# Four shift columns in the high operand, and the norm's sum of squares by one product with ones, in a two-layer diffusion-transformer step

## What is computed

```
h = rms_norm(x, g_mix) * (1 + scale1) + shift1
mo, k, v = mixer(h, w_in, ...)            # differential attention | short convolution, then w_out
x = x + gate1 * mo
h = rms_norm(x, g_ffn) * (1 + scale2) + shift2
x = x + gate2 * ffn(h)                    # SwiGLU in layer 0, top 2 of 8 experts in layer 1
```

## Time and profile before

| | |
|---|---|
| median of 3 runs | 1975.42 us (1972.21 to 1979.14) |
| profiled execution, its own time | 1974.79 us |
| its span | 1972.9 us |
| PE busy | 1910.0 us, 97% of the span, 12579 matmul rows |
| DVE busy | 1117.6 us, 57% |
| ACT busy | 803.2 us, 41% |
| POOL busy | 122.2 us, 6% |
| granted TensorE clock, mean | 0.99 |

### The profile page before, as it was taken

The page is one execution under the profiler, slowest core; times in us unless marked ns, Lnnn a source line. Parts: engine busy times, 40 slices in busy tenths (PEclk is TensorE's granted clock), DMA queues, the critical chain, the costliest instruction groups (busy, mean ns, idle before and its releaser), DMA issues.

```text
span 1972.9 us, 30669 instructions
## 1 busy us (share of the span) xinstructions
PE 1910.0 (97%) x12579; PEld 1748.1 (89%) x12579; DVE 1117.6 (57%) x1799; ACT 803.2 (41%) x1331; POOL 122.2 (6%) x102
## 2 busy tenths in 40 slices
PE   8999889999999999999999899899999999999997
PEld 6999768999999999999997588899898988989885
DVE  2643776444332344437347754476676766768577
ACT  4221364322211222222213644455565655656564
POOL 2000000100000000110000001220000000002210
PEclk8999999999999999999998999899999999999999
DMA  9525100324231431305252011577686776768762
GB/s 348 183 79 205 62 1 22 108 97 181 76 118 43 176 124 65 124 27 192 81 199 53 1 44 39 144 231 244 218 250 212 223 241 204 246 201 303 256 196 73
DMA packets 91699, 290.49 MB, mean 147 GB/s; under 512 B 13236, under 2 KB 21812, under 8 KB 91552
## 3 DMA queue, kind: packets, MB, share of 16 engines
q1 hardware_dynamic: 84416, 270.15, 41.2%
q0 software_dynamic: 7136, 18.30, 2.9%
HBM read 281.98 MB, written 12.28 MB: 149 GB/s over the span
## 4 chain that ended last, share of the span: by engine, by line
PE 90%; DVE 5%; ACT 2%; issue 2%; DMA 1%; SPq 0%; DVEq 0%; ACTq 0%
PE ps L706 47%; PE ps L1056 12%; PE ps L1045 12%; PE ps L1046 6%; PE ps L766 2%; PE ps L891 2%; PE ps L1049 2%; PE ps L882 1%; DVE pr L1995 1%; DVE nbias L1971 1%; PE ps L1048 1%; PE ps L739 1%; DMA ada_raw<-ada_w 1%; PE ps L898 1%; PE ps L1120 1%
## 5 line engine op out<-in xcount | busy, mean ns | idle before, releaser
L1734 DVE TENSOR_TENSOR w_lo<-raw,w_hi 128x1024 fp32r<-128x1024 f32 x394 | 485.2, 1233 | 385.4 <-ACT w_hi L1226 375.7
L1226 ACT ACTIVATE w_hi<-raw 128x1024 fp32r<-128x1024 f32 x394 | 414.4, 1053 | 343.4 <-PE ps L706 172.3
L1045 PE MATMUL ps<-hg,w_hi 128*128 128x416 f32 x1232 | 380.7, 366 | 2.0 <-DVE hg L2152 1.8
L706 PE MATMUL ps<-a_hi,w_hi 128*128 128x320 f32 x1472 | 343.3, 314 | 3.4 <-DVE a_lo L1776 3.4
L706 PE MATMUL ps<-a_lo,w_hi 128*128 128x320 f32 x1472 | 341.0, 313 | 0.0
L706 PE MATMUL ps<-a_hi,w_lo 128*128 128x320 f32 x1472 | 339.9, 312 | 0.0
L1046 PE MATMUL ps<-hg,w_lo 128*128 128x208 f32 x1232 | 319.9, 260 | 0.0
L706 PEld LDWEIGHTS ps<-a_hi,w_hi 128*128 128x128 f32 x1472 | 249.8, 191 | 11.2 <-issue 7.4
L706 PEld LDWEIGHTS ps<-a_hi,w_lo 128*128 128x128 f32 x1472 | 250.9, 190 | 0.0
L706 PEld LDWEIGHTS ps<-a_lo,w_hi 128*128 128x128 f32 x1472 | 250.1, 190 | 0.0
L1045 PEld LDWEIGHTS ps<-hg,w_hi 128*128 128x128 f32 x1232 | 232.8, 189 | 4.3 <-DVE hg L2152 2.0
(11 more groups left out here) (257 smaller groups left out, 2439.3 us busy)
## 6 DMA issues: line engine op xcount, KB each, us to landing
raw<-gu_w SPq DMA_DIRECT2D x220, 512.0 KB
raw<-moe_down_w SPq DMA_DIRECT2D x88, 512.0 KB
ada_raw<-ada_w SPq DMA_DIRECT2D x21, 2048.0 KB, 8.1
raw<-in_w SPq DMA_DIRECT2D x48, 512.0 KB
raw<-down_w SPq DMA_DIRECT2D x22, 512.0 KB
raw<-out_w SPq DMA_DIRECT2D x16, 512.0 KB
ada_pro<-ada_w SPq DMA_DIRECT2D x2, 2048.0 KB, 19.1
y_rows<-ey POOLq DMA_DIRECT2D x7, 512.0 KB
```

The source lines that it names most:

```text
L706: ins = nc.tensor.matmul(out[:, hf, 0:c1 - c0], w, o[:, c0:c1], start=f, stop=e)
L1045: nc.tensor.matmul(sums, whi, both, start=(k == 0), stop=False)
L1226: nc.scalar.activation(w_hi[:, s, :], raw[:, n % RAW, :], ACT.Copy).then_inc(hi_done, 1)
L1734: nc.vector.tensor_tensor(w_lo[:, s, :], raw[:, n % RAW, :], w_hi[:, s, :].bitcast(F32), ALU.subtract)\
```

## The change

The shift columns go into the high operand alone: `a_hi` gets four columns behind the tokens (TA = 644), the high parts of the two shifts and then their low parts, and `a_lo` has 640 columns. The second half of a product is 324 columns wide where the moving operand is high, and 320 where it is low. `scaled` adds the high and the low pair with one reduction over PSUM; for the four q chunks of each layer, which carry a factor, a second operation follows. The scratch that shares memory with the end of the operands keeps its size.

For norms 1 and 2 POOL adds the eighth square too. PE multiplies a full 128x128 matrix of ones by the 640 columns of `ss`, in two fp32 matmuls, before block 4: the sum of each token then stands on every partition at once. ACT takes the root of these 128x640 values into `ss`, and DVE takes the reciprocal of the 128x640 in place, after it has split the third chunk and freed the slot. Sums, diagonal and spread go. Norms 0 and 3 stay as they are.

```diff
-TA = T + 2
+TA = T + 4
...
-            a_lo = sb("a_lo", [P, KB, TA], F32R, c=ops)
+            a_lo = sb("a_lo", [P, KB, T], F32R, c=ops)
...
-                        c0, c1 = (0, HALF) if hf == 0 else (HALF, width)
+                        c0, c1 = (0, HALF) if hf == 0 else (HALF, T if o is opnd_lo else width)
...
+            def norm_total(i):
+
+                g0 = NORM_AT[i][2]
+                open_block(g0)
+                pe.wait_ge(ss_add, KB * (i + 1))
+                for hf in range(2):
+                    ins = nc.tensor.matmul(ps[:, g0 % 4, hf, 0:HALF], ones[:], ss[:, hf * HALF:(hf + 1) * HALF],
+                                           start=True, stop=True)
+                ins.then_inc(mm_done, 1)
...
-                    if norm_i is not None and k == 2:
-                        norm_sums(norm_i)
-                    if norm_i is not None and k == 5:
-                        norm_spread(norm_i)
+                    if norm_i is not None and k == 4:
+                        norm_total(norm_i)
...
+            def keep_root(i):
+
+                n0, q0, g0 = NORM_AT[i]
+                act.wait_ge(mm_done, q0 + 1)
+                nc.scalar.activation(rstd, ps[:, g0 % 4, :, 0:HALF], ACT.Sqrt, bias=eps[:, 0:1], scale=1.0 / D)\
+                    .then_inc(rstd_ready, 1)
...
-                    elif kb == KB - 1:
+                    elif kb == KB - 1 and i in (0, 3):
...
                 dve.wait_ge(rstd_ready, i + 1)
                 dve.sem_inc(blk_free, 1)
+                if i:
+                    link(nc.vector.reciprocal(ss[:], ss[:]))
...
-                nc.vector.tensor_scalar(bcol[:, col, :], ps[:, slot, 1, HALF:HALF + 2], scale, None, ALU.mult)
+                parts = ps[:, slot, 1, HALF:HALF + TA - T].rearrange("p (h c) -> p c h", c=2)
+                if scale == 1.0:
+                    nc.vector.tensor_reduce(bcol[:, col, :], parts, AX, ALU.add)
+                else:
+                    link(nc.vector.tensor_reduce(bcol[:, col, :], parts, AX, ALU.add))
+                    nc.vector.tensor_scalar(bcol[:, col, :], bcol[:, col, :], scale, None, ALU.mult)
                 return nc.vector.tensor_tensor(halves(dst), ps[:, slot, :, 0:HALF], rstd, ALU.mult)
```

More of the change, by code:

```diff
@@ L216, in plan @@
         steps = [("ada", 0, len(ADA_FIRST), 5)] if l == 0 else []
-        steps += [("norm1", 0, 2 * l, l), ("in", chunks, len(items), len(items)),
-                 ("sub", 0, HEADS, None), ("out", OUT_CH, OUT_CH, OUT_CH), ("norm2", 0, 2, 1)]
+        steps += [("norm1", 0, l, l), ("in", chunks, len(items), len(items)),
+                 ("sub", 0, HEADS, None), ("out", OUT_CH, OUT_CH, OUT_CH), ("norm2", 0, 1 + l, 1)]
         if l % 2 == 0:
@@ L269, in hybrid_step @@
             a_hi = sb("a_hi", [P, KB, TA], F32R, c=ops)
-            a_lo = sb("a_lo", [P, KB, TA], F32R, c=ops)
+            a_lo = sb("a_lo", [P, KB, T], F32R, c=ops)
         yab = sb("yab", [P, 2, TT, D])
-        yab_end = sb("yab_end", [P, 2 * KB * (TA - T)])
+        yab_end = sb("yab_end", [P, KB * (TA - T)])
         ht = yab[:, 0]
@@ L403, in hybrid_step @@
         ht_hi = a_hi[:].rearrange("p a b -> p (a b)")[:, 0:T * KB].rearrange("p (t d) -> p t d", t=TT)
-        ht_lo = a_lo[:].rearrange("p a b -> p (a b)")[:, 0:T * KB].rearrange("p (t d) -> p t d", t=TT)
+        ht_lo = a_lo[:].rearrange("p a b -> p (a b)").rearrange("p (t d) -> p t d", t=TT)
         rstd = ss[:].rearrange("p (a b) -> p a b", a=2)
@@ L754, in norm_spread @@
                     fill(NORM_AT[i][2] + 1, FILL["spread"])
-                pe.wait_ge(diag_ready, i + 1)
+                pe.wait_ge(diag_ready, 2 if i else 1)
                 spread(NORM_AT[i][2], diag[:].rearrange("p t c -> p (t c)"))
@@ L1244, in root, with keep_rstd @@
                                      bias=eps[:, 0:1], scale=1.0 / width).then_inc(root_done, 1)
-            def keep_rstd(i):
-                act.wait_ge(mm_done, SPREAD_AT[i] + 1)
-                nc.scalar.activation(rstd, ps[:, NORM_AT[i][2] % 4, :, 0:HALF], ACT.Copy).then_inc(rstd_ready, 1)
+            def keep_rstd():
+                act.wait_ge(mm_done, SPREAD_AT[0] + 1)
+                nc.scalar.activation(rstd, ps[:, NORM_AT[0][2] % 4, :, 0:HALF], ACT.Copy).then_inc(rstd_ready, 1)
+            def keep_root(i):
[3 more added lines that the diff above has]
+                    .then_inc(rstd_ready, 1)
             def gained(i, kb):
@@ L1255, in gained @@
                     act.wait_ge(mod_ready, i + 1)
-                    nc.scalar.activation(a_hi[:, :, T:TA], mods[:, l, 3 * which * KB:(3 * which + 1) * KB, :], ACT.Copy)
+                    nc.scalar.activation(a_hi[:, :, T:T + 2], mods[:, l, 3 * which * KB:(3 * which + 1) * KB, :], ACT.Copy)
                 if i:
@@ L1298, in _ @@
                     take_rows(0, g0)
-                    keep_rstd(0)
+                    keep_rstd()
                     act.wait_ge(mm_done, q0 + ADA_FIRST.index(("turn", 0, 0)) + 1)
@@ L1307, in _ @@
                 else:
-                    root(2 * l, D)
-                    keep_rstd(2 * l)
+                    keep_root(2 * l)
                 n0, q0, g0 = AT[l, "in"]
@@ L1401, in _ @@
                         gained(1, c)
-                root(2 * l + 1, D)
                 if l == 0:
-                    keep_rstd(1)
+                    keep_root(1)
                 else:
+                    root(3, D)
                     modulate()
@@ L1741, in reciprocal_root @@
             def reciprocal_root(i):
-                dve.wait_ge(root_done, i + 1)
+                done = 2 if i else 1
+                dve.wait_ge(root_done, done)
                 link(nc.vector.reciprocal(rms[:, 0, :], rms[:, 0, :]))
@@ L1772, in gained_lo @@
                 if kb == 0:
-                    nc.vector.tensor_tensor(a_lo[:, :, T:TA], mods[:, l, 3 * which * KB:(3 * which + 1) * KB, :],
-                                            a_hi[:, :, T:TA].bitcast(F32), ALU.subtract)
+                    nc.vector.tensor_tensor(a_hi[:, :, T + 2:TA], mods[:, l, 3 * which * KB:(3 * which + 1) * KB, :],
+                                            a_hi[:, :, T:T + 2].bitcast(F32), ALU.subtract)
                 for toks, c in TOKENS_OF:
@@ L1881, in _ @@
                     gained_lo(2, KB - 1, operand[l, "h1"])
-                    reciprocal_root(2)
                 n0, q0, g0 = AT[l, "in"]
@@ L2044, in _ @@
                     gained_lo(1, KB - 1, operand[0, "h2"])
-                    reciprocal_root(1)
                 else:
```

## The result

| | before | changed |
|---|---|---|
| median of the runs | 1976.82 us (4 runs) | 1956.41 us (4 runs) |
| lowest and highest | 1972.21, 1979.14 | 1953.97, 1960.98 |
| profiled execution: span | 1972.9 us | 1956.0 us |

The ratio is 0.9904, with a 95% interval of 0.9886 to 0.9922: about 19 us less, 15 to 23. Timed again later, against 17 runs of the kernel before, the changed kernel had a median of 1960.20 us and a ratio of 0.9916 (0.9895 to 0.9937), 16.6 us less.

A forecast was written before the change was run, and what follows sets the result against it. PE's matmuls were taken to bound the kernel. Norms (-7.46) and product width (-1.8) gave -9.3 us, profiled 1974.79 to 1965.5; with the median 0.6 above, 1966.0 us, range 1960.5 to 1971.5.

The forecast's parts named there:

- The product for the sums and the spread: PE at norms 1 and 2: the new ones-by-640-columns product costs as much as the old spread, 0.84 + 0.24 = 1.08 us.
- The clock behind the sums: PE at norms 1 and 2: 36 matmuls behind the sums lost 1.58 us to a lowered clock; removing the sums regains it.
- POOL's addition: Norms 1 and 2: POOL's extra addition, 1.66 us, ends near 380.4, hidden by 3 us before PE's product at 383.63.
- The reciprocal: DVE at norms 1 and 2: 128x640 takes 4.1 us, costs nothing; PE waits only if it takes over 6.9 us.
- The sum of the columns: DVE's `bcol` reduction of four values: about 159 ns, q chunks one more operation of 0.16 us; cost taken as nothing.
- Width of the products: Dense and input chunks on PE: two matmuls of 324 replace three of 322, 2.5 ns less in 736 products, 1.8 us less.
- the rival in which the excess goes: Chunk products: extra columns cost only 0.46 ns each, width part 6.8 us less, 1961.1 us in all; chance 15%.
- the norms' term: PE at norms 1 and 2: sums (2.15) and slow stretch (1.58) go, 3.73 us less each, 7.46 in all.
- Price by columns: Chunk products: each extra column costs 2.15 ns, so width adds 3.2 us, 1971.1 us in all; chance 10%.
- the width has no price of its own: Chunk products: the 0.31 us comes from something else and stays, columns add 0.7 us, 1968.6 in all; chance 12%.
- the clock still falls behind the product: Norm 1, norm 2 or both: clock falls behind the new product, 1.6 us each, 1968 to 1969.5 us; chance 8%.
- the slower case: Norms 1 and 2: PE waits for DVE's reciprocal past 6.9 us; at 15 us it gives 1982 us; chance 5%.

The follow-up runs named there:

- norm only: Kernel before with only norms 1 and 2 changed, operands still 642 columns wide; timed twice: medians 1971.56 and 1971.40 us, ratios 0.9972 and 0.9973.
- columns only: Kernel before with only the operands' new form (shift columns in the high operand), sums, spread and diagonal kept; median 1968.82 us, ratio 0.9961.

## Why the prediction was right on the norms and wrong on the size

- **The product for the sums and the spread: right.** Priced at 1.08 us, it stands in the chain of the changed kernel with 1.08 and adds 1.14 to its stage. The stages were to last 15.4 us and last 15.2.
- **The clock behind the sums: right for the profiled pair, wrong as a term of the median.** Of the 7.46 us, 2 x 1.58 were the fall of the clock, taken as certain because it fell behind three of three sets in one execution. Over the profiles here it fell behind 3 of 10 at norms 1 and 2. The part that every profile shows is 4.3 us; two series of norm only brought 5.5 and 5.3, whose intervals hold both 4.3 and 7.3.
- **POOL's addition: right.** 3 us of cover were forecast, 3.3 are there.
- **The reciprocal: right.** 4.1 us taken from two small forms, 4.15 measured. Root, split and scaling came at 384.86, 386.64 and 391.96, forecast 384.91, 386.60 and 392.0. PE doesn't wait. The room at norm 1 was under-counted (2.8 against 4.6), because the rows of the modulation, 1.86 us on PE ahead of the fourth chunk, were left out; at norm 2 it was 3.0 against 2.7.
- **The sum of the columns: right.** 161 ns a reduction, and PE waits no longer.
- **"Width of the products": this step failed.** It read the 4.3 ns that a 322 cost over a 320 as a price "for being wider than 320 at all", kept it for the 324, and so had 1.8 us less. Measured are 9.2 us less, five times that (the chunk of `columns only` takes 7.04 us), and more than the rival in which the excess goes (6.8), since that still charged the new columns. The reading from the down projection was sound as far as it went: those matmuls run at 146.7 ns, and so do these now. What it lacked is that the down projection differed in two things, 320 columns and rows 640 apart. The prediction weighed width, columns, or neither, and never named the distance; in the kernel before each of the two is worth some 0.05 us a chunk. The change moved both. By what rule they act stays open.

Against 7.46 + 1.8 = 9.3 forecast stand 7.3 + 9.2 = 16.5 in the pair of traces, and the timed series had 19.0 and 16.6. That the norms' term came out right to 0.2 us is luck in part: it rests on two falls of the clock that most other profiles don't have. "Price by columns" and "the width has no price of its own" are ruled out by the chunk of 7.04 us, "the clock still falls behind the product" by 0 of 26 cases, the slower case by the 4.15 us. The range was too narrow on the gain's side: its end was a rival in which columns still cost, when nothing in the rows forbade that they cost nothing.

## What to carry to other kernels

When two stages run the same matmuls at different speed, list every way in which their operands differ (width, distance between rows, place) and give each its own case before a price goes to one of them; a row length of 640 or 644 in place of 642 was worth as much here as the width. What a profile shows once of the granted clock is one draw: count it as a certain gain only if several executions show it. The room behind a new instruction on a side engine is its end to the start of the work that needs it, with all that the bounding engine does in between, and what passes beyond that room can cost more than the wait itself: here the clock was down behind both waits, 1.6 and 2.1 us on top of 3.7 and 5.7.

## What the runs showed of the hardware that was not expected

- The distance between the starts of successive moving operands has a price: at 320 columns of this type 148.3 ns a matmul with steps of 2, 322 or 642, 147.5 with 4, 324 or 644, 146.7 with 8, 320, 640 or 648. A shift of all starts by 8 bytes had none (the chunk stayed at 7.040 us).
- The time of a matmul goes in uneven steps with its width: 140.0 ns at 304 and at 312, 146.7 at 320, 153.3 from 328 to 336. A 320 is thus 13.3 ns over its columns at 2.4 GHz.
- Behind some two microseconds of one-column matmuls between dense work the clock fell in 3 of 10 cases, and within one execution it fell at one place and held at another with the same instructions.
- Behind a wait of PE of 3.7 us and one of 5.5 us the granted clock was 0.61 and 0.51, and the next chunk took 1.6 and 2.1 us longer.
- A reciprocal of 128x640 fp32 on DVE takes 4.15 us, 6.5 ns an element of a row, the slope that 1, 5 and 20 elements had the earlier trace rows.
